# Three moves in a hand-written order of TensorE tasks: an attention transpose ahead of a weight product, and modulation steps at other places

## The reference

```
for l in range(DEPTH):                       # DEPTH = 2
    h = x @ w_in[l]                          # split into q, f, i, gate, cq, ckv, kr, gate, mem_q, gate
    y_hg  = _hgrn2_group(...)                # 8 heads, chunked gated recurrence
    y_mla = _mla_group(...)                  # 8 heads, causal softmax attention
    y_mem = _memory_group(...)               # 4 heads, attention to mem
    y = concat(y_hg * silu(g0), y_mla * silu(g1), y_mem * silu(g2)) @ w_out[l]
    x = _layernorm(DEEPNORM_ALPHA * x + y, ln_g[l], ln_b[l])
```

## Time and profile before

| what | value |
|---|---|
| device time, median of 3 runs | 1416.79 us (1416.4 to 1417.09) |
| the profiled execution | 1416.4 us, its span 1414.6 us |
| PE busy | 1277.5 us, 90% of the span |
| VectorE busy | 818.0 us, 58% |
| GpSimd busy | 651.8 us, 46% |
| ScalarE busy | 412.3 us, 29% |
| DMA | 407.84 MB, mean 288 GB/s |
| granted TensorE clock, mean | 0.966 |

### The profile page before, as it was taken

One profiled execution on the slowest core, in us unless ns is written; L12 is line 12 of the kernel. 1 busy time (PEld: TensorE's weight loads), 2 busy tenths in 40 slices (PEclk: granted clock), 3 DMA queues, 4 the chain that ended last, 5 costly groups with the idle time before them and its releaser, 6 DMA issues.

```text
span 1414.6 us, 17530 instructions
## 1 busy us (share of the span) xinstructions
PE 1277.5 (90%) x6312; PEld 788.6 (56%) x6312; DVE 818.0 (58%) x1681; ACT 412.3 (29%) x1030; POOL 651.8 (46%) x643
## 2 busy tenths in 40 slices
PE   9999999999999999999998899958967888777786
PEld 8887686548886777559566556523323333333332
DVE  1766287340666377350448756889797654554545
ACT  1533334201342333121314323332313231212123
POOL 0556667423446766504004354535645455454540
PEclk9999999999999999999999999979999989999999
DMA  9544344634444254543628999999999999999995
GB/s 373 206 164 180 120 165 168 262 131 183 164 180 173 96 233 177 195 176 141 271 86 329 421 417 415 421 421 421 421 421 421 421 423 421 422 422 421 422 421 209
DMA packets 53888, 407.84 MB, mean 288 GB/s; under 512 B 6165, under 2 KB 8618, under 8 KB 11306
## 3 DMA queue, kind: packets, MB, share of 16 engines
q0 software_dynamic: 36864, 268.45, 45.9%
q1 hardware_dynamic: 15850, 137.23, 25.2%
q10 hardware_dynamic: 1088, 1.05, 0.3%
HBM read 404.58 MB, written 1.07 MB: 287 GB/s over the span
## 4 chain that ended last, share of the span: by engine, by line
PE 28%; DMA 24%; DVE 6%; issue 3%; ACT 2%; POOL 1%; ACTq 0%; DVEq 0%; POOLq 0%
PE bank L1119 10%; DMA ring<-in_peer_uv,vM 7%; DMA yT<-in_peer_uv,vM 7%; PE pj L729 6%; PE pj L693 4%; DMA hv<-in_peer_uv,vM 4%; DMA more_rows<-in_peer_uv,vM 3%; DMA qM<-in_peer_uv,vM 3%; PE pj L989 2%; PE pj L708 2%; DVE tri L1871 1%; DMA qvE<-in_peer_uv,vM 1%; PE bank L999 1%; ACT rope L1338 1%; DVE big L1871 1%
## 5 line engine op out<-in xcount | busy, mean ns | idle before, releaser
L693 PE MATMUL pj<-xT,ring 128*128 128x256 f32 (+1 forms) x1568 | 318.4, 363 | 0.9 <-ACT hv L1276 0.4
L693 PEld LDWEIGHTS pj<-xT,ring 128*128 128x128 f32 x1568 | 276.6, 190 | 36.5 <-issue 2.6
L607 POOL TENSOR_SCALAR more_rows<-more_rows,lbt 128x256 f32<-128x256 f32 x168 | 176.0, 1048 | 16.4
L641 POOL DMA_INDIRECT ring<-in_peer_uv,vM x101 | 122.5, 1213 | 120.9 <-PE bank L1119 109.5
L729 PE MATMUL pj<-ring,yT 128*128 128x512 f32 x320 | 141.1, 595 | 0.0
L605 POOL TENSOR_SCALAR mod_part<-more_rows,lbt 128x256 f32<-128x256 f32 x24 | 23.7, 989 | 246.6 <-issue 122.1
L1336 ACT ACTIVATE rope<-vM 128x4 f32<-128x4 f32 (+3 forms) x84 | 17.1, 204 | 405.6 <-DVE big L1871 323.0
L608 POOL TENSOR_TENSOR mod_part<-mod_part,more_rows 128x256 f32<-128x256 f32 x168 | 127.9, 761 | 14.0
L1119 PE MATMUL bank<-ring,causal 128*128 128x512 f32 x200 | 99.9, 638 | 19.2 <-ACT causal L1344 19.2
L1119 PE MATMUL bank<-ring,tri 128*128 128x512 f32 x204 | 99.4, 627 | 19.4 <-ACT tri L1344 19.4
L729 PEld LDWEIGHTS pj<-ring,yT 128*128 128x128 f32 x320 | 59.7, 190 | 69.5 <-issue 69.2
(11 more groups left out here) (369 smaller groups left out, 2114.0 us busy)
## 6 DMA issues: line engine op xcount, KB each, us to landing
ring<-in_units SPq DMA_DIRECT2D x44, 2048.0 KB, 9.5
more_rows<-in_w_ada SPq DMA_DIRECT2D x24, 1024.0 KB, 4.9
ring<-in_units SPq DMA_DIRECT2D x2, 1536.0 KB, 7.8
ring<-in_peer_uv,vM POOLq DMA_INDIRECT x101, 23.1
memT<-in_mem SPq DMA_DIRECT2D x2, 512.0 KB, 5.3
ring<-in_units SPq DMA_DIRECT2D x1, 1024.0 KB, 9.0
xT<-in_x_turned SPq DMA_DIRECT2D x1, 1024.0 KB, 10.7
x<-in_x SPq DMA_DIRECT2D x1, 1024.0 KB, 16.0
```

What stands on the lines that cost most here:

```text
L607: do(g.tensor_scalar(mod_w[:, c, :], mod_w[:, c, :], silu_c[:, c:c + 1], None, ALU.mult))
L641: pool.indirect_dma_start(row_slot[k], None, d["peer_uv_2"], bass.IndirectOffsetOnAxis(ap=expert[:, t, j:j + 1], axis=0))\
L693: ins = nc.tensor.matmul(pj[s][0:n, 2 * m + first:2 * m + stop], ring[:, slot, at:at + n], act[:, c, first:stop], start=(c == 0), stop=(c ...
```

## The change

Only the words of two tables move. Both first-block layers get the same three edits on PE:

1. Place one: `GMa P0 AD GMb Y0` becomes `P0 GMa AD Y0 GMb`.
2. Place two: `Y2 AD Y3 AD P4` becomes `Y2 AD AD Y3 P4`.
3. Place three: `Y8 AD L15 LD L16 O0t L17 Y9 O0u` becomes `Y8 L15 LD L16 O0t L17 Y9 AD O0u`. This is AD8 in layer 0 and AD20 in layer 1. In `DVE_ORDER` the matching step moves from before `L15` to behind `L17`.

```diff
-PE_ORDER = ["""... AD S2 GMa P0 AD GMb Y0 L03 Q1a L04 Q1b S3
+PE_ORDER = ["""... AD S2 P0 GMa AD Y0 GMb L03 Q1a L04 Q1b S3
...
-    Da15 Da16 S9 Da17 P9 Y7 Db15 Db16 L14 Y8 AD L15 L16 Db17 L17 Da18 Db18 L18 Y9 HO2 AD HO3 HN2 AD HN3 AD LN"""
+    Da15 Da16 S9 Da17 P9 Y7 Db15 Db16 L14 Y8 L15 L16 Db17 L17 AD Da18 Db18 L18 Y9 HO2 AD HO3 HN2 AD HN3 AD LN"""
```

More of the change, by code:

```diff
@@ L50 @@
 N_MOD_PIECES = N_MOD * D_MODEL // MOD_COLS
[L58 to L65, removed]
+PE_ORDER = ["""MKa MKb C VEC F0 N Q0 LD UQ KR F1a UK LD UV S0 F1b L01 S1 L02 AD S2 P0 GMa AD Y0 GMb L03 Q1a L04 Q1b S3
+            P1 L05 Y1 LD AD I0a P2 LD L06 LD S4 S5 P3 I0b Y2 AD AD Y3 P4 MV Y4 L07 P5 G0a L08 LD Y5 LD AD G0b MQ LD
+            AD HO0 S6 HO1 HN0 L11 GEa AD P6 S7 GEb S8 HN1 L12 LD I1 Y6 L13 P7 P8 S9 L14 Y7 G1a G1b P9 Y8 L15 LD L16
+            O0t L17 Y9 AD O0u LD L18 O2t HO2 HO3 AD HN2 AD O2u LD HN3 O3t AD O1t O3u O1u""",
+            """MKa Xt MKb Xu MKc C F0 N Q0 LD UQ KR F1a UK LD UV S0 F1b L01 S1 L02 AD S2 P0 GMa AD Y0 GMb L03 Q1a L04 Q1b S3
+            P1 L05 Y1 LD AD I0a P2 LD L06 LD S4 S5 P3 I0b Y2 AD AD Y3 P4 MV Y4 L07 P5 G0a L08 LD Y5 LD AD G0b MQ LD
+            AD HO0 S6 HO1 HN0 L11 GEa AD P6 S7 GEb S8 HN1 L12 LD I1 Y6 L13 P7 P8 S9 L14 Y7 G1a G1b P9 Y8 L15 LD L16
+            O0t L17 Y9 AD O0u LD L18 O2t HO2 HO3 AD HN2 AD O2u LD HN3 O3t AD O1t O3u O1u""",
             """Xt BUt BKt Xu MT BUu BKu BQa BQb SK S0 S1 BVa S2 PL0 PL1 BVb P0 P1 S3 S4 Y0 S5 Y1 O1t P2 O0t P3 Y2 P4 Y3 P5 Y4
```

## The result

| | before | changed |
|---|---|---|
| device time, median of 7 runs on the same chip | 1417.0 us (1416.03 to 1421.77) | 1427.01 us (1423.89 to 1428.15) |
| ratio, with its 95% interval | | 1.0053 (1.0038 to 1.0068) |
| the profiled execution, its span | 1416.4 us, 1414.6 us | 1422.7 us, 1420.9 us |
| PE busy | 1277.5 us | 1274.7 us |
| start of the expert layer's first indirect load | 743.16 us | 748.97 us |

The ratio means 7.5 us, within 5.4 and 9.6 by its interval, where 3.5 were forecast; by the medians it is 10. The record lists ten more executions of the changed kernel, 1420.21 to 1426.55 us; with them its median is 1424.85, which is 1.0055 of 1417.0. The measured 1427.01 us lies above the forecast range of 1417.8 to 1423.4. The profiled executions are 6.3 us apart. Both spans end 671 to 672 us behind the first indirect load, so the time was lost ahead of it, as assumed.

What follows compares the result with a forecast made beforehand. PE's list was taken as the path up to 743 us, the DMA's rate after it. Terms 1.75 + 0.15 + 0.8 + 0.8 = 3.5 us gave 1420.3 us by the median, range 1417.8 to 1423.4.

Steps and rivals of the forecast that it cites:

- Place one, the wait: P0 ahead of GMa, both layers: P0 waits 2.2 us for its bank, until VectorE's first L02 blend ends.
- the fall: Rival: the granted clock falls behind P0's wait, 1.5 us in each layer, 6.5 us in all, 1423.3; chance 0.08.
- signs of being wrong: PE not stopping at P0, over 2 us of wait at AD11 or O1t, or granted clock 0.5 behind P0.
- The reason given against it: Against a clock fall: AD19's 1.67 us wait lies where the clock was 1.00; P0's wait stands between long busy products.
- VectorE can't be earlier: At P0's wait: VectorE works through without a pause, so the 2.2 us cannot shrink.
- Nothing added: Behind place one: the gate comes about 2.9 us later, but L04's 1.85 us of room covers the extra 0.7.
- Place two: AD4 ahead of Y3: the delay from P0 removes AD4's 0.45 us wait, so layer 0 keeps 1.75 us.
- layer 1 keeps 0.15: Layer 1: the waits of 0.38 at AD16 and 1.67 at AD19 take 2.05 of P0's 2.2 us.
- Place three: AD8 behind Y9: POOL's pieces 10 and 11 end later, a new 0.8 us wait at AD11, again in layer 1.
- O1's weights: Behind AD11: their delayed load lands at 293.9 against a need at 295.8, about 1.9 us of room.
- only from slice 21 on: Profile page's slices: DMA engines reach nine tenths from there; before about 743 us DMA is not the limit.
- a shift at 743 us goes to the end one for one: Last stage, after 743 us: it runs at the DMA's rate, so the whole delay reaches the end; 0.04 that it is lost.

Runs made afterwards that it cites:

- place one filled: Place one alone plus nine extra 128x128 matmuls on PE ahead of P0, against the kernel before: 1418.62 us, ratio 1.0023.
- changed filled: The whole change plus nine extra 128x128 matmuls on PE ahead of P0, against the kernel before: 1420.78 us, ratio 1.0037.
- blend first: The whole change with VectorE's L02 blend ahead of its step Da03, against the kernel before: 1419.2 us, ratio 1.0023.
- second execution: The unfilled changed kernel profiled again, against the kernel before: median 1422.53 us, ratio 1.0052; its profiled distance is +8.61 us.
- third and fourth: Two more profiled executions of the unfilled changed kernel, one execution each: 1425.87 and 1424.35 us.
- Y0 alone: Only Y0 moved ahead of GMb, P0 left behind GMa, against the kernel before: 1415.5 us, ratio 1.0002.
- places two and three: Only the edits of places two and three, without place one, against the kernel before: 1417.34 us, ratio 1.0013.
- place one alone: Only the edit of place one (P0 ahead of GMa, Y0 ahead of GMb), both layers, against the kernel before: 1420.6 us, ratio 1.0031.
- P0 behind S1: P0 moved further forward, right behind S1, with Y0 ahead of GMb, against the kernel before: 1427.18 us, ratio 1.0087.

## Why the prediction was right in direction and too small

**Place one, the wait.** Right: 1.99 us of idle, in both layers, for VectorE's line 1654, and P0 starts 3.80 us behind AD0, where GMa started 1.64 behind it before; 2.16 us of delay against 2.2.

**Place one, what follows it.** This is the step that failed. The sum had "2.2 us" for P0 and no term for the clock; the fall stood among the rivals, at 0.08, with 1.5 us a time. It is the common case, seven of eight, and costs about 1.7 us a time (from P0's start to GMa's end 9.20 to 9.23 us, against 7.53 or 7.54 with the clock up). A granted clock of 0.5 behind P0 was among the prediction's own signs of being wrong. Where the idle time is filled, or cut to 0.38, GMa takes 7.07 in all six chances (place one filled, changed filled, blend first). The reason given against it was that a wait of 1.67 us at AD19 had left the clock up, and that P0's wait stands between long products. Neither argument held: a wait only 0.3 us longer, at this place, was followed by a fall. Whether the length or the place makes the difference was not tested. "VectorE can't be earlier" didn't hold either: with the blend ahead of Da03, P0 started 2.15 us behind AD0 (90.85 to 93.00) and not 3.80.

**"Nothing added" behind the gate.** Half right. With the clock up it holds: P2 doesn't wait in the filled kernels. With the gate 1.7 us later still, P2 waits 0.68 us in layer 0 (0.56 in the second execution, none in the third and fourth), and in layer 1 0.34 to 0.39 where the clock fell there. VectorE's own lines show how. Before:

```profile
128.59 0.69 DVE L1640 TENSOR_TENSOR big<-big,kT 128x512 f32<-128x512 f32 x1 [2.46 <-ACT big L1238]
129.32 0.69 DVE L1641 TENSOR_TENSOR big<-big,qT 128x512 f32<-128x512 f32 x1
```

Changed:

```profile
131.86 0.89 DVE L1640 TENSOR_TENSOR big<-big,kT 128x512 f32<-128x512 f32 x1 [2.46 <-ACT big L1238]
132.79 1.23 DVE L1641 TENSOR_TENSOR big<-big,qT 128x512 f32<-128x512 f32 x1
```

Both pairs start at the same distance from ScalarE's work. But the pair now runs beside POOL, which starts its piece there at 130.72, and takes 2.12 us in place of 1.38. The Trainium skill ("SBUF — State Buffer", section "Who interferes with whom") says that a VectorE instruction with two SBUF inputs and a GpSimd one that reads SBUF lock each other out; this trace agrees, with those 0.74 us. In the changed kernel filled, the pair runs at 130.88 and takes 0.69 twice; POOL's first instruction starts beside its second half, at 131.73, and it is POOL's that takes 1.36 us there in place of 0.93. In the third execution, where P2 doesn't wait, POOL starts later and the pair takes 1.54:

```profile
131.84 0.93 POOL L605 TENSOR_SCALAR mod_part<-more_rows,lbt 128x256 f32<-128x256 f32 x1 [5.83 <-DMA more_rows<-in_w_ada]
...
132.36 0.69 DVE L1640 TENSOR_TENSOR big<-big,kT 128x512 f32<-128x512 f32 x1 [2.46 <-ACT big L1238]
133.09 0.85 DVE L1641 TENSOR_TENSOR big<-big,qT 128x512 f32<-128x512 f32 x1
```

**Place two.** Right in layer 0: AD4's wait of 0.45 is gone. In layer 1 AD16's 0.38 is gone, but of the 1.67 us at AD19, on which "layer 1 keeps 0.15" rested, the filled kernel gave back only 0.96. That wait is not stable: 1.67 and none in two executions of before, 1.51 with Y0 alone, none with places two and three. I took one execution's longest wait for a fixed credit.

**Place three.** Right: 0.8 us was forecast at AD11 and AD23, 0.90 and 0.96 came, and 0.76 to 0.84 in the other kernels that have it. O1's weights gave no wait, as reckoned.

**The account.** The profiled execution: layer 0, P0's delay 2.16, the fall 1.68, P2 0.68, AD11 0.90, less AD4's 0.45: 4.97 us, against 5.01 measured. Layer 1, without a fall: 2.16 + 0.96 - 0.38 - 1.67 = 1.07, against 1.41.

Held against the filled kernel's 4.52 us, the other executions say what the falls are worth. The table adds up what is seen on PE: the falls; the waits of P2 and of the recurrence; those of AD11 and AD23 over the filled kernel's; less AD19's 0.71 us, a wait that the filled kernel has and none of the others. The last row is place one alone against place one filled, where AD19 waits 0.63.

| execution | sum of the terms | measured |
|---|---|---|
| changed, profiled, one fall | 1.68 + 0.68 + 0.28 - 0.71 = 1.93 | 1.90 |
| changed, second, two falls | 3.37 + 0.56 + 0.34 + 0.58 - 0.02 - 0.71 = 4.12 | 4.09 |
| changed, third, two falls | 3.35 + 0.39 - 0.06 - 0.71 = 2.97 | 3.06 |
| changed, fourth, two falls | 3.39 + 0.36 - 0.03 - 0.71 = 3.01 | 3.09 |
| place one alone, two falls | 3.27 + 0.63 + 0.34 - 0.63 = 3.61 | 3.76 |

So two falls with all that goes with them are worth 3 to 4 us of the distance: 3.3 to 3.4 the falls themselves, up to 1.5 what they make late, less the 0.7 at AD19. Whether the falls cover that wait or it is one that comes and goes can't be told: it is missing in layer 1 of the profiled execution too, where the clock didn't fall. The terms that the prediction had are the rest, 4.5 us by the filled kernel, where it had 3.5.

**A reading beside it.** The prediction says that the DMA engines reach nine tenths "only from slice 21 on". In the earlier trace rows slice 21 has 2, slice 22 has 8, and 9 stands from slice 23 on. Nothing in the sum rests on it.

**What stays open.** Part of the time lies outside the distance. The second profiled execution took 1426.61 us, 10.2 more than the first of before: 8.61 of it in the distance, and 1.5 in the stage behind the first indirect load (672.9 us against 671.4). That stage takes 670.0 to 673.5 us over all the profiled executions. The two of before have the two shortest, 671.4 and 670.0; two executions can't tell whether that is chance. So "a shift at 743 us goes to the end one for one" is shown to no better than some 3 us. The upper half of the first series of the changed kernel is 10 to 11 us above its before, more than any distance seen. Which executions of a series have falls could only be seen in the profiled ones. Why seven of the eight waits were followed by a fall and one was not is open too. No kernel tried beats the one before.

## What to carry to other kernels

Before a task is moved forward, look up who reads the last user of its result bank, and who will get its own bank next: the move of P0 cost 2 us at its own wait, and one place further 4.4 us at another task. Price a new wait of 2 us on a busy TensorE with the clock behind it: here 2.16 us of delay drew 1.7 more behind them, and then what the delay made late. A wait that is to absorb a delay must be there in more than one execution.

## What the runs showed of the hardware

An idle time of 2.0 us ahead of a busy product brought the granted clock down (0.56 and 0.59 in 94 to 96 and 96 to 98 us, 1.00 before and behind), in seven of eight cases of the changed kernel and both of place one alone; a fall came behind the 4.38 us of "P0 behind S1" too, in both layers. That the idle time is the cause is shown by the six cases in which it was filled or cut to 0.38 us, all without a fall. Idle times of 0.63 us (Y0 alone) were not followed by one either, nor was the 1.67 us at AD19. Length alone doesn't decide, though. The expert layer of the kernel before has a longer wait with no fall; first PE's line, then the windows around it:

```profile
762.58 1.96 PE L1119 MATMUL bank<-more_rows,tri 128*128 128x512 f32 x4 [2.93 <-ACT tri L1344]
```

```profile
759.00:761.00 2.00, 0.65 (x6) 0.46 (x5) 1.97 (x4) 0.00 (x0) 1.05 (x1) 1.00 1.04 438
761.00:763.00 2.00, 0.42 (x1) 0.30 (x2) 1.90 (x7) 1.28 (x5) 0.75 (x1) 1.00 0.61 193
763.00:765.00 2.00, 2.00 (x6) 0.95 (x5) 2.00 (x13) 1.93 (x10) 0.19 (x1) 1.00 0.97 389
```

PE stood for 2.93 us and went on at 1.00. What sets these cases apart was not tested. Plain matmuls on ones in the gap kept the clock up in all four chances, and P0 started no later for them (94.42 against 94.43 us).

VectorE's pair of two-input instructions took 1.38 us alone and 2.12 beside POOL; where POOL's instruction started second, it was POOL's that grew, from 0.93 to 1.36 us.
